# Two decoder blocks on one core: where the weight splits stand, who adds the weight sums, and how the first output rows are tiled

## What is computed

```python
def swiglu_2(x, w_gate, w_up, w_down):
    return (jax.nn.silu(x @ w_gate) * (x @ w_up)) @ w_down

for l in range(2):
    x = layer_norm(ALPHA * x + 0.5 * swiglu_2(x, ffn1_gate[l], ffn1_up[l], ffn1_down[l]), ...)
    h = x @ w_in[l]
    ...
    mix = concatenate([y_pool, y_hgrn]) @ w_out[l]
    x = layer_norm(ALPHA * x + mix, ...)
    x = layer_norm(ALPHA * x + 0.5 * swiglu_2(x, ffn2_gate[l], ffn2_up[l], ffn2_down[l]), ...)
```

## Time and profile before

| | us |
|---|---|
| median of 3 runs | 2984.46 |
| the runs | 2984.46, 2991.61, 2981.26 |
| profiled execution | 2986.32 |
| its span, first to last instruction | 2984.5 |
| PE busy | 2843.9 (95%) |
| DVE busy | 1702.1 (57%) |
| ACT busy | 1172.7 (39%) |
| POOL busy | 1116.8 (37%) |

### The profile page before, as it was taken

The page is one execution under the profiler, slowest core; times in us unless marked ns, Lnnn a source line. Parts: engine busy times, 40 slices in busy tenths (PEclk is TensorE's granted clock), DMA queues, the critical chain, the costliest instruction groups (busy, mean ns, idle before and its releaser), DMA issues.

```text
span 2984.5 us, 41884 instructions
## 1 busy us (share of the span) xinstructions
PE 2843.9 (95%) x17509; PEld 2467.9 (83%) x17509; DVE 1702.1 (57%) x2021; ACT 1172.7 (39%) x1577; POOL 1116.8 (37%) x993
## 2 busy tenths in 40 slices
PE   9999999999999899999988998989999999899999
PEld 8888886788888899788767998879987887699977
DVE  5544344453432877634646877358874463688743
ACT  4333245642322544325235444244442424354432
POOL 0115617011100766310516664147752032476520
PEclk9999999999999999999999999999999999999999
DMA  4223223123223232222121232223322221223222
GB/s 151 94 97 99 92 75 91 57 85 96 95 99 99 77 100 96 87 94 85 58 71 64 94 99 86 98 71 100 99 93 87 88 81 53 66 87 99 94 91 78
DMA packets 77643, 263.10 MB, mean 88 GB/s; under 512 B 12240, under 2 KB 12368, under 8 KB 77456
## 3 DMA queue, kind: packets, MB, share of 16 engines
q1 hardware_dynamic: 77456, 260.43, 26.7%
HBM read 257.12 MB, written 2.10 MB: 87 GB/s over the span
## 4 chain that ended last, share of the span: by engine, by line
PE 72%; POOL 8%; DVE 7%; DMA 6%; issue 4%; ACT 3%; SPq 0%; ACTq 0%; DVEq 0%; POOLq 0%
PE bank L393 16%; PE bank L394 16%; PE bank L395 15%; DMA praw<-weight_pairs 5%; PE bank L581 4%; PE bank L585 4%; PE bank L583 4%; POOL praw L2372 2%; POOL praw L2377 2%; PE bank L530 2%; ACT phi L1006 1%; DMA wraw<-weights 1%; PE bank L459 1%; POOL praw L2380 1%; PE bank L463 1%
## 5 line engine op out<-in xcount | busy, mean ns | idle before, releaser
L1589 DVE TENSOR_TENSOR wlo<-wraw,whi 128x1024 fp32r<-128x1024 f32 x311 | 404.3, 1311 | 470.2 <-ACT whi L990 470.0
L990 ACT ACTIVATE whi<-wraw 128x1024 fp32r<-128x1024 f32 x319 | 332.1, 1055 | 550.4 <-DMA wraw<-weights 550.3
L393 PE MATMUL bank<-Ah,whi 128*128 128x512 f32 x1056 | 420.1, 398 | 26.5 <-DVE Al L1672 21.0
L393 PE MATMUL bank<-H,whi 128*128 128x512 f32 x984 | 393.8, 400 | 32.4 <-DVE wlo L1589 24.4
L395 PE MATMUL bank<-Al,whi 128*128 128x512 f32 x1056 | 415.6, 394 | 0.0
L394 PE MATMUL bank<-Ah,wlo 128*128 128x512 f32 x1056 | 415.6, 394 | 0.0
L581 PE MATMUL bank<-TF,plo 128*128 128x256 f32 x1280 | 370.4, 289 | 29.1 <-DVE cb L1651 18.5
L394 PE MATMUL bank<-H,wlo 128*128 128x512 f32 x984 | 389.1, 395 | 0.0
L395 PE MATMUL bank<-H,whi 128*128 128x512 f32 x984 | 388.8, 395 | 0.0
L583 PE MATMUL bank<-TF,phi 128*128 128x256 f32 x1280 | 364.0, 284 | 0.0
L585 PE MATMUL bank<-TF,phi 128*128 128x256 f32 x1280 | 363.9, 284 | 0.0
(11 more groups left out here) (352 smaller groups left out, 5418.0 us busy)
## 6 DMA issues: line engine op xcount, KB each, us to landing
wraw<-weights SPq DMA_DIRECT2D x319, 512.0 KB, 3.5
praw<-weight_pairs SPq DMA_DIRECT2D x160, 512.0 KB, 3.5
X<-x_t SPq DMA_DIRECT2D x8, 256.0 KB, 6.9
y_t<-X SPq DMA_DIRECT2D x8, 256.0 KB, 2.0
dist<-attention SPq DMA_DIRECT2D x4, 256.0 KB, 4.0
wraw<-weights SPq DMA_DIRECT2D x2, 256.0 KB, 4.1
Y<-masks SPq DMA_DIRECT2D x1, 512.0 KB, 8.7
zsum<-attention SPq DMA_DIRECT2D x2, 256.0 KB, 3.3
```

The source lines that it names most:

```text
L393: pe.matmul(b, sh, mh, start=start, stop=False)
L990: act.activation(whi[:, u % NS, :], wraw[:, u % NS, :], ACT.Copy).then_inc(*S.done("weights_hi", ("hi", u)))
L1589: dve.tensor_tensor(wlo[:, u % NS, :], wraw[:, u % NS, :], f32(whi[:, u % NS, :]), SUB).then_inc(*S.done("weights_lo", ("lo", u)))
```

## The change

Five edits, all in the second model's part.

1. **Positions after the mixer.** The calls of `hi_to` and `lo_to` in the out product of the mixer count the 12 blank tiles now: the ends of rows move by 12 tiles, and the calls before them from p + 3, p + 11 and p + 19 to p + 15, p + 23 and p + 31.
2. **Two of the four weight sums on DVE.** The operation of 512 elements moves from POOL to DVE (`two_sums`); POOL waits for it and does the third and fourth.
3. **The low parts.** `pair_lo` is cut in two: `pair_lo` and `sum_lo`. With k = 3 the seven block additions stand between them, and the sums of the next pair unit come behind `sum_lo`. ACT copies the first product inside `pair_hi`, between the two high parts.
4. **Two rows side by side.** In the down product of the paired FFNs rows 0 and 1 run together, k by k, in two banks; the weight stream is laid out to match.
5. **Splits of the result.** POOL makes `Al` of k = 4 and 5 alone, DVE those of 6 to 21; `hi_to` and `lo_to` in `late_a` start at k = 10 and go by two tiles per k.

```diff
+    def two_rows(name):
+        plan.extend((name, k, c) for k in range(NF) for c in range(2))
+        plan.extend((name, k, c) for c in range(2, KD) for k in range(NF))
...
+        def two_rows(st):
+
+            bs = [open_bank((st, "row", nb), True) for nb in range(2)]
+            for k in range(NF):
+                pe.wait_ge(*S.at(("Ah", st, k)))
+                pe.wait_ge(*S.at(("Al", st, k)))
+                for nb in range(2):
+                    hi, lo, ends = tile()
+                    mm3(bs[nb][:, :], hi, lo, Ah[:, k, :], Al[:, k, :], k == 0, k == NF - 1,
+                        ends + ((("full", (st, "row", nb)),) if k == NF - 1 else ()))
...
+            if s % 4 == 1 and s > 1:
+                first_product(PAIRED[v // N_PAIRS], s // 4 * 2)
             act.wait_ge(*S.at(("sums", v)))
             act.activation(phi[hi_slot][:, 6:14, :], praw[raw][:, 8:16, :], ACT.Copy).then_inc(
                 *S.done("weights_hi", ("sum hi", v)))
...
             for j in range(KEPT, NF):
-                hi_to(p + j)
-                if j == NF - 4:
+                if j > 9:
+                    hi_to(p + 2 * j - 16)
+                if j == 9:
                     silu_pair(st, NF - 2)
                 split_a(st, j)
...
-            hi_to(p + 3)
+            hi_to(p + 15)
...
                 if h == 1:
-                    hi_to(p + 4 + 7)
-            hi_to(p + 4 + 15)
-            ends = [p + 20 + 4 * (nb + 1) if nb < 4 else p + 36 + KD * (nb - 3) for nb in range(KD)]
+                    hi_to(p + 16 + 7)
+            hi_to(p + 16 + 15)
+            ends = [p + 32 + 4 * (nb + 1) if nb < 4 else p + 48 + KD * (nb - 3) for nb in range(KD)]
...
+        def two_sums(v):
+            raw = praw[pair_slots(v)[0]]
+            dve.wait_ge(pair_in[pair_slots(v)[0]], 16 * pair_landings(v))
+            dve.tensor_tensor(raw[:, 8:12, :].rearrange("p (f e) n -> p f (e n)", f=2),
+                              raw[:, 2:6, :].rearrange("p (f e) n -> p f (e n)", f=2),
+                              raw[:, 0:2, :].rearrange("p e n -> p (e n)").unsqueeze(1).to_broadcast([P, 2, 2 * P]),
+                              ADD).then_inc(*S.done("sums_two", ("two sums", v)))
...
+            two_sums(v0)
             for k in range(4):
                 dve.wait_ge(*S.at(("TF hi", st, k)))
...
             pair_lo(v0)
+            sum_lo(v0)
+            two_sums(v0 + 1)
             pair_lo(v0 + 1)
+            sum_lo(v0 + 1)
+            two_sums(v0 + 2)
...
                         pair_lo(v0 + s + 2)
                     elif s >= N_PAIRS - 2:
                         lo(u0 + 4 + s - N_PAIRS + 2)
+                    if k == 3:
+                        blocks(st, j)
+                    if 0 < s < N_PAIRS - 2:
+                        sum_lo(v0 + s + 2)
+                    if 0 < s < N_PAIRS - 3:
+                        two_sums(v0 + s + 3)
                     if k == 0 and j > 2:
                         product(st, j - 2)
...
-                    if k == 3:
-                        blocks(st, j)
...
-            for j in range(KEPT, NF):
-                lo_to(p + j)
-                if j == NF - 4:
+            for j in range(KEPT + 2, NF):
+                if j > 9:
+                    lo_to(p + 2 * j - 16)
+                if j == 9:
                     product(st, NF - 2)
-                if j % 3:
-                    split_a(st, j)
+                split_a(st, j)
...
         def pair_sums(v):
             raw = praw[pair_slots(v)[0]]
-            pool.wait_ge(pair_in[pair_slots(v)[0]], 16 * pair_landings(v))
-            pool.tensor_tensor(raw[:, 8:12, :].rearrange("p (f e) n -> p f (e n)", f=2),
...
             pool.wait_ge(*S.at(("two sums", v)))
```

More of the change, by code:

```diff
@@ L104, in stream_plan @@
         groups((f"gate2_{l}",) * 2 + (f"up2_{l}",) * 2, (0, 1, 0, 1))
-        rows(f"down2_{l}", NF, KD)
+        two_rows(f"down2_{l}")
     assert len(plan) == N_TILES
@@ L1131, in ffn_pairs, with first_product @@
                             split_a(st, i)
[L1132 to L1136 removed]
+            first_product(st, NF - 2)
+        def first_product(st, j):
+            act.wait_ge(*S.at(("full", ((st, j), 0))))
+            act.wait_ge(*S.at(("product", st, j - 1)))
+            act.activation(cb[:, 0, :], bank(((st, j), 0))[:, :], ACT.Copy).then_inc(
+                *S.done("rows_out", ("first product", st, j), empties=[((st, j), 0)]))
         def scale_rows(st, k):
```

43 lines of the change are left out of this document (22 added, 21 removed).

## The result

| | before | after |
|---|---|---|
| median, us | 2983.48 (2981.26 to 2991.61, 4 runs) | 3026.41 (3024.87 to 3029.41, 4 runs) |
| span of the profiled execution | 2984.5 | 3027.6 |
| ratio, 95% interval | | 1.0144 [1.0119, 1.0161] |

The kernel became 1.4% slower. I cut both traces at three marks in each paired FFN: F, the last matmul ahead of the FFN's first column pair; P, the first pair matmul (both by their starts); E, the end of the last pair matmul.

What follows compares the result with a forecast made beforehand. PE was taken to bound the kernel throughout, with DVE becoming the bound in the pair loop. 2986.3 - 33 - 42 + 29 + 86 = 3026, median 1.9 lower, so 3024 us; own range 2990 to 3055, whole range 2935 to 3080.

Steps and rivals of the forecast that it cites:

- part 3: Start of the pairs: POOL's first sums wait for DVE behind the normalization, with the token sums queued behind; +29 us.
- part 4: Pair loop: serial over DVE and POOL, 23.8 us per j against PE's 20.0; +86 us for four FFNs.
- Part 1: Positions behind the mixer: units split a row earlier take away most waits for late weight splits; -33 us.
- part 2: Down products: two rows side by side and the new split order cover 10.5 us per FFN, four times; -42 us.
- Rival C: Pair loop: PE waits drop the clock at each j, 1.5 us more per j, +54, about 3078 us; chance 0.13.
- A: Pair loop: the POOL step hides and the loop follows PE at 20.0 us per j, 2888 us; chance 0.07.
- B: Pair loop stays as long as before, only parts 1 to 3 count, 2938 us; chance 0.14.
- D: Start of the pairs: part 3 costs nothing, the token sums being bound by X anyway, 2995 us; chance 0.08.

## Why the prediction was right

The mechanisms were right, and that the total is only 2 us off is in part luck: against the table above part 3 was 7 us too large, part 4 12 too small, parts 1 and 2 together 3 too small, the stretch ahead of them 1 longer, and most of this cancels.

**Part 1** (-33) measured -35 alone, **part 2** (-42) measured -44 alone. The mechanisms were the ones named: waits for weight splits in the mixers of 1.1 us at most, no wait in rows 0 and 1, and the half clock at the gap of 3.9 us gone. One reading was loose: of the 6 us in which 12 matmuls stand in the earlier trace rows, the first 0.7 are the end of the wait, so they took 5.3.

**Part 3** (+29) measured +21.6 from F to P. The step from the end of H to PE was right, 20.0 us against 20.2. What was off is the end of H: with POOL idle, DVE's low parts there are no longer contended (0.69 each, where one of the earlier trace rows took 1.23), so H ends at 994.5 in a0 and not at 996.8, and PE's wait in front of the pairs is 13.1 to 13.7 and not 15. The kernel that gives POOL the first unit's sums back shows it: there H's last low part in a0 takes 1.23 again. I had moved POOL's work away and kept the durations that it had caused. Taking edit 2 out, wholly or for the first unit, gives 23.7 and 26.1 in this phase, near the measured and not the forecast figure.

**Part 4** (+86) measured +98.4, the right mechanism and a loop 2.2 us longer per FFN (239.2 on average, 237.0 forecast); the rest of the difference is that the loop of before was 214.6 on average, and I took a0's 215.4 for all. The chain of 4.6 us is 4.58 in the trace, the 23.8 us of one j 23.86, DVE's waits of about 1.7 are 1.73 and 1.74. Of its three parts the first is 25.2 and not 26.2, the eight j are 191.6 and not 190.4, and the last is the mis-sized one: 22.4 in the mean and not 20.4, with a wait and half clock at its start.

**The waits of PE.** I expected about 3 us per j. They are 66.4 / 36 = 1.8, and 3.5 at the longest. Much of the rest of PE's slack goes into half clock. In a0 PE resumes behind a wait of 1.78 us, and in the stretch behind it (1137.30 to 1141.00, above) 17 matmuls take 3.7 us, at a granted clock of 0.55, where 17 x 0.119 = 2.0:

```profile
1137.32 0.39 PE L585 MATMUL bank<-TF,plo 128*128 128x256 f32 x1 [1.78 <-DVE cb L1699]
```

That is a loss of 1.7 that no list of waits shows: 20.2 + 1.8 + 1.7 = 23.7. It goes so in eight of the nine j behind the first in a0, in eight in b0 and in all nine in b1, but in a1 only in three. There one whole j, with a wait of 2.8 us and one of 0.3 in it, looks like this:

```profile
2132.10:2155.90 23.80, 20.64 (x168) 20.24 (x168) 16.71 (x21) 8.61 (x10) 6.77 (x8) 1.00 0.27 89
```

Where the clock stays full for a whole j, PE waits for the 3 us that I expected; where it falls, the half clock eats the wait. The distances of the block additions are the same 23.8 in both, and the loop is as long in a1 as in b1. So to cost the half clock at nothing for the end, as the prediction did, was right: DVE sets the pace. Rival C (the half clock breaks through) falls by that.

**The rivals.** A (the POOL step hides) and B (the loop as long as before) fall with the distances of the block additions. A's 20 us per j came only in the kernel where POOL's step is hidden beside the block additions. D (part 3 costs nothing) falls with the +21.6, and with the 30 us that its undoing gave.

The rule that sends elementwise work to VectorE (the Trainium skill, GPSIMD Engine Reference, When to use GPSIMD) has the price right: a sum of 256 elements is 0.42 us on DVE and 0.74 on POOL. The price did not decide between the two engines here. With the first unit on POOL, all other sums on DVE give 2893 us and all sums on POOL 2890; half of the chain on each gives 3001.

**What stays open.** Whether the 3.0 us ahead of the mixer's out product, which stand in all kernels as "issue", can go; this wasn't tried. The kernel with all sums on DVE missed its expectation by 31 us. That DVE's own work was what bound it is shown by the kernel that takes 1.64 us per j from DVE, whose loop fell from 210.7 to 204.4; that each sum's wait for the one before it makes the 0.2 us per pair unit is read from the trace, and no run tests it.

## What to carry to other kernels

When a step of a chain moves to another engine, look at what stands between it and the operation that waits for the chain's end: with nothing between, both engines work in turn, and less work takes longer (DVE and POOL together 234 us busy in a loop of 239, against 312 in one of 215 before). Move the whole chain, or start its first step at least as early as the partner's time plus two handoffs, beside work with which the partner does not contend. And ask what is queued behind the new wait on the other engine: here 16 token sums, 20 us at each start.
